# Two mixers of a three-layer network: pooled features made feature-major, moving sums by shifted additions in place of band matmuls

## The chip, the cores and the metric

One core of a Trainium2 chip runs the whole program. The time is device microseconds for one execution; lower is better. TensorE multiplies, VectorE, ScalarE and GpSimd (called POOL in the rows) do elementwise work, and SP issues most of the loads.

## The reference, cut to what matters

The network has two hybrid layers and a third of another kind, on 256 tokens and 1024 features, in float32. The change is in the first two layers' mixers, in the projection u and the pooling of it:

```python
h = rms_norm(x, mix_norm)
z = h @ w_in
u, q, k, v, gl = z[..., :512], z[..., 512:1024], ...
y_pool = multiscale_pool(u, pool_w, pool_scale)
y_attn = moba_attention(rope(rms_norm(q)), rope(rms_norm(k)), v)
merged = gates[0] * (y_pool @ w_branch_pool) + gates[1] * (y_attn @ w_branch_attn)

def multiscale_pool(u, w_grp, scale):      # u: 256 tokens, 4 groups of 128 features
    for g, w in enumerate((2, 4, 8, 16)):
        lo = max(t + 1 - w, 0)             # causal moving mean over w tokens
        mean = (csum[t + 1, g] - csum[lo, g]) / (t + 1 - lo)
    d = pooled - u
    y = einsum('bsgc,gcd->bsgd', d, w_grp) # a 128x128 product per group
    return y * scale
```

## The kernel before

Every weight matrix comes in tiles of 128 x 1024 (512 KB), in the order of `tile_plan`. Each tile is split into a high and a low part: ScalarE copies it to `whi` with rounding (L1362), VectorE subtracts that from the tile and writes `wlo` (L1971). A product is then three matmuls, high x high, high x low and low x high. Six split tiles exist at a time. ScalarE works at most five tiles ahead of TensorE and VectorE four (`ahead`; three or so in the gates), and a new tile may take a buffer when TensorE has finished the tile six before it.

There are two forms of product. `group` (by `group_part`, L760, L761, L765) makes the result token-major: 256 tokens are two halves `a`, each with a PSUM bank of 512 feature columns, and one weight tile serves two of the eight input blocks. `feat_block` (L723, L724, L730) makes it feature-major: the weight tile is the stationary side, the 256 tokens are the columns, and one tile gives 128 features over all eight input blocks. The wide form (L739, L746) is that of the gates.

A mixer of layer 0 or 1 (`mixer1`) runs the groups k, q, u, v (four tiles each) and then sixteen gate tiles, the two branch products and the output product. TensorE, ScalarE and VectorE each have their own program and go through the same tiles; in each of them `tick` counts beats, two to a tile, so that q holds beats 1 to 8, u 9 to 16, v 17 to 24 and the gates begin with 25. Small work is hung on the beats. In the kernel before:

- beats 10 and 12: TensorE transposes k (L1062), ScalarE evicts it (L1693). Beats 20 and 22: the same for q (L1691).
- beats 11 and 13: VectorE multiplies q by the cosine table (L2295), 15 and 16: it adds the sine part (L2324), which GpSimd has made in four products (L2661, L2662), after a few small operations for the norm (L2666 to L2674).
- beats 17, 19, 21, 23 (`pool_diff`): TensorE multiplies the token-major `us` with band matrices (`poolm`, 1536 columns of constants), which gives the mean minus u, feature-major (L1108, L1109), in float32. ScalarE evicts it to `dT` (L1699).
- beats 18, 20, 22, 24 (`pool_mix`): TensorE multiplies `dT` with the group's 128x128 matrix (L1118), ScalarE evicts the high part with the scale (L1705), VectorE the low part (L2328, semaphore `yplo`).
- beat 26: the first attention scores on TensorE (L998); they wait for all four `yplo`.

`pool_mix(g)` writes bank `side[2 + g % 2]`, so groups 2 and 3 wait until VectorE has evicted groups 0 and 1:

```python
if g >= 2:
    E.wait_ge("yplo", 4 * l + g - 1)
```

Each engine goes through its program in order; an instruction that waits holds all behind it on its engine. The order of a VectorE `tick` before the change is: q by cosine, q addition, `pool_mix`, attention.

Of the kernel before, what the change touches and what calls it, by code (L numbers as in the profile page):

```python
# [15 lines left out]
P = 128  # L16
S = 256
# [13 lines left out]
def constants():  # L31
    c = {}
    c["ident"] = np.eye(P, dtype=np.float32)
    t = np.arange(P)
    tri = np.where(t[None, :] > t[:, None], np.float32(NEG), np.float32(0)).astype(np.float32)
    c["cmask"] = np.concatenate([tri, np.zeros((P, P), np.float32), tri], 1)
    c["bigT"] = np.where(t[:, None] > t[None, :], np.float32(1e30), np.float32(0)).astype(np.float32)
    half = 32
    inv = (np.float32(1.0) / (np.float32(10000.0) ** (np.arange(half, dtype=np.float32) * np.float32(2.0 / 64)))).astype(np.float32)
    ang = (np.arange(S, dtype=np.float32)[:, None] * inv[None, :]).astype(np.float32)  # L40
    cos, sin = np.cos(ang).astype(np.float32), np.sin(ang).astype(np.float32)
    cs = np.concatenate([cos, cos], 1).reshape(2, P, 64)
# [3 lines left out]
    pm = []  # L46
    tt = np.arange(S)
    for w in (2, 4, 8, 16):
        lo = np.maximum(tt + 1 - w, 0)
        cnt = (tt + 1 - lo).astype(np.float32)  # L50
        s = np.arange(S)[:, None]
        m = np.where((s >= lo[None, :]) & (s <= tt[None, :]), np.float32(1) / cnt[None, :], np.float32(0))
        m = m - np.eye(S)
        pm += [m[0:P, :], m[P:S, P:S]]
# [100 lines left out]
def tile_plan():  # L155
# [100 lines left out]
class Counts:  # L256


    def __init__(self, plan):
# [31 lines left out]
        for st, tag in enumerate(STAGES):  # L291
            groups = [f"{tag}p"] if tag in FFNS else [tag + g for g in (("k", "q", "u", "v") if tag != "M" else ("k3", "nq", "v3", "mv", "mo"))]
# [25 lines left out]
    def banks(self):  # L318
# [37 lines left out]
        for st, tag in enumerate(STAGES):  # L356
# [20 lines left out]
            if tag != "M":  # L377
# [5 lines left out]
                for a in range(2):  # L383
                    claim((f"{tag}u", a), "u_ev", 2 * m + a + 1)
# [31 lines left out]
def build_program(nc, x_in, wstream, gains, const_in, par_in, out, cat, pat, plan, addends):  # L416
# [3 lines left out]
    with ExitStack() as ctx:  # L420
# [43 lines left out]
        kT1, v1, us = arena[:, 3328:4352], arena[:, 4352:5376], arena[:, 6400:7424]  # L464
        qT1 = arena[:, 2304:3328]
        dT, tab1, poolm, pw = arena[:, 7424:7680], arena[:, 7680:8192], arena[:, 8192:9728], arena[:, 9728:10240]
# [54 lines left out]
        PES = ["tile", "tok", "xt", "ft", "acc", "qkt_t", "pl_d", "pl_w", "score", "pT", "pv",  # L521
               "kT_t", "lg_row", "lg_col", "c_hT", "c_w2", "c_rep", "c_sc", "c_pT", "pv_c", "ml_s", "ml_h", "ml_t", "turn"]
        ACTS = ["w_hi", "sq", "xhi", "tok_a", "act", "hidhi", "pad", "qk_ev", "hst_sq", "kt_ev", "qt_ev", "u_ev", "v_ev", "dT", "yphi", "ex", "g_low",
                "pT_ev", "low", "yahi", "gate", "k3_ev", "kc2_ev", "kT_ev", "nq_ev", "v3_ev", "mqk_ev", "lg_ln", "lg_ex", "c_part", "c_hc",
                "c_kv", "c_exp", "c_pTe", "conv_t", "mv_ev", "ml_e", "ml_sq", "m_yhi", "mo_ev", "tokp", "tokv", "sil", "xf_hi"]
        DVES = ["sq_v", "xhi0", "w_lo", "x", "xn", "xlo", "tok_m", "mul", "hidlo", "cv", "mrg", "hst_rd", "rp_n", "rp_c", "rp_add", "yplo",
                "mx", "nrm", "g_sum", "yalo", "gfin", "sum", "lg_d", "lg_cp", "c_fold", "c_v", "c_s", "conv_q", "conv_k", "ml_k", "ml_p", "ml_d", "ml_n", "ml_g", "m_ylo", "gmo", "xf", "xf_lo", "comb", "tokm"]
        POOLS = ["mh", "rstd", "hb", "tab", "zero", "kst", "qst", "rp_s", "X", "warm", "cvp", "c_z", "ml_r", "padz", "rowz", "kz", "vz", "xz"]
# [71 lines left out]
        def sp_program(E):  # L600
# [88 lines left out]
        def pe_program(E):  # L689
# [393 lines left out]
            def mixer1(s, l):  # L1083
# [14 lines left out]
                def pool_diff(g):  # L1098
                    E.wait_ge("u_ev", 2 * l + 2)
                    E.wait_ge("ld_pw", 32 * l + 32)  # L1100
                    if g < 2:
                        E.wait_ge("kt_ev", 2 * l + g + 1)
                    else:
                        E.wait_ge("qt_ev", 2 * l + g - 1)
                        E.wait_ge("dT", 4 * l + g - 1)
                    b, pm = side[g % 2], poolm[:, g * 384:g * 384 + 384]
                    reach = P + 2 ** (g + 1)
# [4 lines left out]
                def pool_mix(g):  # L1112
                    E.wait_ge("dT", 4 * l + g + 1)
                    if g >= 2:
                        E.wait_ge("yplo", 4 * l + g - 1)
                    else:
                        E.wait_ge("x", 4 * (s - 1) + 3 + g)
                    e.matmul(side[2 + g % 2][:, 0:S], pw[:, g * P:g * P + P], dT, start=True, stop=True).then_inc(sem["pl_w"], 1)  # L1118

                def before(i):  # L1120
                    if i < 2:
                        E.wait_ge("dT", 4 * l + 3 + i)
                        E.wait_ge("kt_ev", 2 * l + 2)
                        E.wait_ge("qt_ev", 2 * l + 2)
                        E.wait_ge("yplo", 4 * l + 4)
                    else:
                        E.wait_ge("v_ev", 2 * l + 2)

                def tick():
# [6 lines left out]
                    if beat in (17, 19, 21, 23):  # L1136
                        pool_diff((beat - 17) // 2)
# [5 lines left out]
                for g in ("q", "u", "v"):  # L1143
                    group(f"{tag}{g}", 512, tick)
# [193 lines left out]
        def act_program(E):  # L1338
# [329 lines left out]
            def mixer1(s, l):  # L1668
# [26 lines left out]
                def pool_diff(g):  # L1695
                    E.wait_ge("pl_d", 4 * l + g + 1)
                    if g:
                        E.wait_ge("pl_w", 4 * l + g)
                    e.activation(dT, side[g % 2][:, 0:S], ACT.Copy).then_inc(sem["dT"], 1)  # L1699

# [6 lines left out]
                def tick():  # L1707
# [6 lines left out]
                    if beat in (17, 19, 21, 23):  # L1714
                        pool_diff((beat - 17) // 2)
# [7 lines left out]
                for g in ("q", "u", "v"):  # L1723
                    for k0, _ in a_group(512):
# [5 lines left out]
                    for a in range(2):  # L1730
# [4 lines left out]
                        if g == "u":  # L1735
                            e.activation(us[:, a * 512:a * 512 + 512], b[:, :], ACT.Copy).then_inc(sem["u_ev"], 1)
                        else:
                            e.activation(v1[:, a * 512:a * 512 + 512], b[:, :], ACT.Copy).then_inc(sem["v_ev"], 1)
# [223 lines left out]
        def dve_program(E):  # L1962
# [334 lines left out]
            def mixer1(s, l):  # L2297
# [27 lines left out]

                def pool_mix(g):
# [4 lines left out]
                def tick():  # L2331
# [18 lines left out]
                for g in ("q", "u", "v"):  # L2350
                    for k0, _ in a_group(512):
# [279 lines left out]
        def pool_program(E):  # L2631
# [67 lines left out]
            def prepare1(s, l):  # L2699
# [6 lines left out]
                e.tensor_scalar(hb16, PR(f"bg{l}"), 0.5, None, ALU.mult).then_inc(sem["hb"], 1)  # L2706
                rope_tables(tab1[:, 0:256], PR(f"kn{l}"), 1, 2 * l + 1)
# [149 lines left out]
def pack_weights(I, plan, addends, total):  # L2857
# [37 lines left out]
    for l in range(2):  # L2895
# [3 lines left out]
        for j, nm in enumerate("uqkv"):  # L2899
            group(f"L{l}{nm}", wi[:, j * 512:(j + 1) * 512])  # L2900
# [96 lines left out]
```

## Time and profile before

| what | value |
|---|---|
| median of 3 runs | 1406.26 us (1406.22 to 1406.81) |
| the profiled execution | 1406.52 us, span 1404.5 us |
| granted TensorE clock, mean | 1.000 |
| busy: TensorE matmul, VectorE, ScalarE, GpSimd | 1398.6, 1089.2, 862.0, 229.6 us |
| instructions | 20175 |

The span is the time from the first to the last instruction in the profile; the profiled execution took 2.0 us more than it. Matmuls overlap, so a matmul's own duration is longer than the step from its start to the next one's; steps are the measure of what it costs.

### The profile page before, as it was taken

To read this page: it belongs to the slowest core of one execution; us is meant where nothing else is said; L and a number is where in the kernel's file an instruction comes from. 1 tells how busy PE (TensorE), PEld (TensorE's weight loads), DVE (VectorE), ACT (ScalarE), POOL (GpSimd) and SP (SyncE) were. 2 spreads that over 40 slices of the span, in tenths; PEclk is the share of its full clock that TensorE was granted. 3 is DMA by queue.
4 is the path that set the end of the run, shared out by engine and by line. 5 is a ranking of instruction groups with operands and counts; after the bars stand their busy time and mean duration, and the time that the engine had idled before them with its cause. 6 is when DMAs were issued, how large, how long until landed. Compare 5 with 4: busy or idle time off the path is not lost.

```text
span 1404.5 us, 20175 instructions
## 1 busy us (share of the span) xinstructions
PE 1398.6 (100%) x7624; PEld 1195.2 (85%) x7624; DVE 1089.2 (78%) x1650; ACT 862.0 (61%) x1397; POOL 229.6 (16%) x307
## 2 busy tenths in 40 slices
PE   9999999999999999999999999999999999999999
PEld 7888888898888888888888888888888899888887
DVE  7878876776978878788775778788777878678776
ACT  6657656755657657675567646666567765455553
POOL 1112133000111001112050001114149200100000
PEclk9999999999999999999999999999999999999999
DMA  9999755464999859998564557999547336456551
GB/s 369 301 299 279 220 204 176 136 197 180 304 258 289 211 190 300 273 273 223 194 223 149 169 181 270 267 275 259 188 154 250 126 121 216 160 174 216 192 185 58
DMA packets 84200, 305.75 MB, mean 218 GB/s; under 512 B 9348, under 2 KB 9480, under 8 KB 84104
## 3 DMA queue, kind: packets, MB, share of 16 engines
q1 hardware_dynamic: 69992, 253.33, 50.8%
q0 software_dynamic: 13824, 50.34, 18.8%
q8 instruction: 61, 1.00, 0.3%
q10 hardware_dynamic: 288, 0.79, 0.2%
q14 instruction: 35, 0.29, 0.1%
HBM read 303.37 MB, written 1.05 MB: 217 GB/s over the span
## 4 chain that ended last, share of the span: by engine, by line
PE 98%; DVE 1%; DMA 0%; ACT 0%; issue 0%; POOL 0%; DVEq 0%; ACTq 0%; POOLq 0%
PE bank L739 18%; PE bank L746 9%; PE bank L693 9%; PE bank L694 9%; PE bank L695 9%; PE bank L899 5%; PE bank L898 5%; PE bank L902 5%; PE bank L760 4%; PE bank L765 4%; PE bank L761 4%; PE bank L723 3%; PE bank L730 3%; PE bank L724 3%; PE bank L713 1%; PE bank L998 1%
## 5 line engine op out<-in xcount | busy, mean ns | idle before, releaser
L1971 DVE TENSOR_TENSOR wlo<-raw,whi 128x1024 fp32r<-128x1024 f32 x409 | 492.2, 1231 | 12.3 <-ACT whi L1362 12.2
L1362 ACT ACTIVATE whi<-raw 128x1024 fp32r<-128x1024 f32 x409 | 417.5, 1048 | 19.0 <-PE bank L695 12.4
L739 PE MATMUL bank<-hx,whi 128*128 128x512 f32 x1088 | 268.6, 393 | 0.0
L739 PEld LDWEIGHTS bank<-hx,whi 128*128 128x128 f32 x1088 | 200.4, 188 | 41.3 <-issue 2.0
L693 PE MATMUL bank<-whi,hid 128*128 128x512 f32 x536 | 211.1, 394 | 0.0
L694 PE MATMUL bank<-wlo,hid 128*128 128x512 f32 x536 | 209.2, 390 | 0.0
L695 PE MATMUL bank<-whi,hid 128*128 128x512 f32 x536 | 208.8, 389 | 0.0
L746 PEld LDWEIGHTS bank<-hx,wlo 128*128 128x128 f32 x1088 | 142.9, 191 | 7.7
L746 PE MATMUL bank<-hx,wlo 128*128 128x256 f32 x1088 | 145.2, 282 | 0.0
L1971 DVE TENSOR_TENSOR wlo<-gates,whi 128x1024 fp32r<-128x1024 f32 x96 | 116.1, 1221 | 5.6 <-ACT whi L1362 5.1
L695 PEld LDWEIGHTS bank<-whi,hid 128*128 128x128 f32 x536 | 100.6, 188 | 21.4
L1362 ACT ACTIVATE whi<-gates 128x1024 fp32r<-128x1024 f32 x96 | 100.5, 1056 | 26.8 <-PE bank L695 13.8
L693 PEld LDWEIGHTS bank<-whi,hid 128*128 128x128 f32 x536 | 100.9, 188 | 18.9
L694 PEld LDWEIGHTS bank<-wlo,hid 128*128 128x128 f32 x536 | 100.9, 188 | 18.4
L1391 ACT ACTIVATE hid<-prod 128x256 fp32r<-128x256 f32 x78 | 32.6, 418 | 122.0 <-DVE prod L2280 58.6
L2683 POOL DMA_DIRECT2D gates<-w_dram x64 | 56.0, 874 | 288.0 <-DVE wlo L1971 287.6
L760 PE MATMUL bank<-whi,hx 128*128 128x512 f32 (+1 forms) x256 | 101.9, 399 | 0.9 <-DVE hx L1999 0.9
L761 PE MATMUL bank<-whi,hx 128*128 128x512 f32 (+1 forms) x256 | 98.1, 384 | 0.0
L765 PE MATMUL bank<-wlo,hx 128*128 128x512 f32 (+1 forms) x256 | 77.4, 385 | 0.0
L2638 POOL TENSOR_SCALAR small<-small 128x1 f32<-128x1 f32 x15 | 10.7, 716 | 403.5 <-ACT arena L1377 403.5
L898 PE MATMUL bank<-whi,yhi 128*128 128x512 f32 x192 | 75.2, 392 | 0.0
L899 PE MATMUL bank<-whi,ylo 128*128 128x512 f32 x192 | 74.9, 390 | 0.0
(298 smaller groups left out, 2375.0 us busy)
## 6 DMA issues: line engine op xcount, KB each, us to landing
raw<-w_dram SPq DMA_DIRECT2D x414, 512.0 KB, 4.5
gates<-w_dram POOLq DMA_DIRECT2D x64, 512.0 KB, 8.0
gates<-w_dram SPq DMA_DIRECT2D x32, 512.0 KB, 5.5
arena<-w_dram POOLq DMA_DIRECT2D x32, 512.0 KB, 9.0
arena<-w_dram SPq DMA_DIRECT2D x16, 512.0 KB, 5.1
gain<-g_dram SPq DMA_DIRECT2D x7, 512.0 KB, 3.3
arena<-c_dram SPq DMA_DIRECT2D x2, 768.0 KB, 6.2
out_dram<-x SPq DMA_DIRECT2D x4, 256.0 KB, 2.0
```

The costliest lines, as they stand in the source:

```text
L693: e.matmul(psum, shi, mhi, start=first, stop=False, skip_group_check=True)
L694: e.matmul(psum, shi, mlo, start=False, stop=False, skip_group_check=True)
L695: return e.matmul(psum, slo, mhi, start=False, stop=last, skip_group_check=True)
L739: e.matmul(b[:, :], hi_of(j)[:, k * P:k * P + P], hx[:, k * 2 * S:k * 2 * S + 2 * S], start=k == 0, stop=False, skip_group_check=True)
L746: ins = e.matmul(b[:, 0:S], lo_of(j)[:, k * P:k * P + P], hiT(k), start=False, stop=k == KD - 1, skip_group_check=True)
L760: e.matmul(b[:, 0:n], hiT(k, a * P, a * P + P), w, start=k == 0, stop=False, skip_group_check=True)
L761: e.matmul(b[:, 0:n], loT(k, a * P, a * P + P), w, start=False, stop=False, skip_group_check=True)
L765: ins = e.matmul(b[:, 0:n], hiT(k, a * P, a * P + P), w, start=False, stop=k == KD - 1, skip_group_check=True)
L898: e.matmul(b[:, :], sh(k), half(hi_of(j), k), start=k == 0 and n not in (2, 4), stop=False, skip_group_check=True)
L899: e.matmul(b[:, :], sl(k), half(hi_of(j), k), start=False, stop=False, skip_group_check=True)
L1362: e.activation(hi_of(t), raw_of(t), ACT.Copy).then_inc(sem["w_hi"], 1)
L1971: e.tensor_tensor(lo_of(t), raw_of(t), hi_of(t).bitcast(F32), ALU.subtract).then_inc(sem["w_lo"], 1)
```

## The change

The u projection becomes feature-major: four tiles of one group of 128 features each, by `feat_block`, evicted by ScalarE to `u4`, 16 columns of zeros ahead of the 256 tokens of each group. VectorE makes the moving sums from it by repeated doubling: a sum over 2 is u plus u shifted by 1, a sum over 4 that plus itself shifted by 2, and so on, so group g needs g + 1 additions. A small product mends the first w tokens, whose mean is over fewer, and a last operation takes sum / w minus u and writes it into `u4`, where TensorE's `pool_mix` reads it. The band matmuls, their evictions and their constants go. On VectorE the new `pool_diff(g)` is hung on beats 12, 14, 16 and 18, behind the q work of the beat and ahead of `pool_mix`. GpSimd sets the zeros in the stage before.

```diff
@@ constants
-    c["pool"] = np.concatenate(pm, 1).astype(np.float32)
+    tt = np.arange(16)
+    c["pool"] = np.broadcast_to(np.concatenate([np.float32(w) / np.minimum(tt + 1, w).astype(np.float32) for w in (2, 4, 8, 16)])[None, :], (P, 64)).astype(np.float32)
@@ tile_plan
+            if g == "u":
+                plan.extend((f"L{l}u{f}", TW, True) for f in range(4))
+                continue
@@ banks
-                for a in range(2):
-                    claim((f"{tag}u", a), "u_ev", 2 * m + a + 1)
+                for f in range(4):
+                    claim((f"{tag}u", f), "u_ev", 4 * m + f + 1)
@@ SP, load_pool_w
-                e.dma_start(poolm, const_in[:, cat["pool"][0]:cat["pool"][1]]).then_inc(sem["ld_pw"], 16)
+                e.dma_start(poolc, const_in[:, cat["pool"][0]:cat["pool"][1]]).then_inc(sem["ld_pw"], 16)
@@ TensorE, mixer1
-                def pool_diff(g):
-                    ...
-                    e.matmul(b[:, 0:reach], us[:, g * P:g * P + P], pm[:, 0:reach], start=True, stop=False, skip_group_check=True)
-                    e.matmul(b[:, P:S], us[:, 512 + g * P:512 + g * P + P], pm[:, S:S + P], start=False, stop=True,
-                             skip_group_check=True).then_inc(sem["pl_d"], 1)
                 def pool_mix(g):
-                    E.wait_ge("dT", 4 * l + g + 1)
+                    E.wait_ge("pl_d", PLD(l, g))
...
-                    e.matmul(side[2 + g % 2][:, 0:S], pw[:, g * P:g * P + P], dT, start=True, stop=True).then_inc(sem["pl_w"], 1)
+                    e.matmul(side[2 + g % 2][:, 0:S], pw[:, g * P:g * P + P], u4[:, g, 16:16 + S], start=True, stop=True).then_inc(sem["pl_w"], 1)
...
-                for g in ("q", "u", "v"):
-                    group(f"{tag}{g}", 512, tick)
+                group(f"{tag}q", 512, tick)
+                for f in range(4):
+                    feat_block(T[f"{tag}u{f}"], claim((f"{tag}u", f))[:, 0:S], tick=tick)
+                group(f"{tag}v", 512, tick)
@@ ScalarE, mixer1
+                        for f in range(4):
+                            ahead(T[f"{tag}u{f}"])
+                            tick()
+                            tick()
+                            E.wait_ge("tile", DONE[f"{tag}u{f}"])
+                            E.wait_ge("uz", l + 1)
+                            e.activation(u4[:, f, 16:16 + S], bank[K.BANK[f"{tag}u", f][0]][:, 0:S], ACT.Copy).then_inc(sem["u_ev"], 1)
@@ VectorE, mixer1
+                def pool_diff(g):
+                    n = PLD(l, g) - (g + 3)
+                    u, s_ = u4[:, g, :], u4[:, g, :]
+                    E.wait_ge("u_ev", 4 * l + g + 1)
...
+                    for i in range(g + 1):
+                        d, o = 2 ** i, part_sum[i % 2]
+                        if n:
+                            E.wait_ge("pl_d", n)
+                        e.tensor_tensor(o[:, 2 * d - 1:], s_[:, 2 * d - 1:], s_[:, d - 1:16 + S - d], ALU.add).then_inc(sem["pl_d"], 1)
+                        s_, n = o, n + 1
+                    w = 2 ** (g + 1)
+                    E.wait_ge("ld_pw", 32 * l + 32)
+                    E.wait_ge("pl_d", n)
+                    e.tensor_tensor(s_[:, 16:16 + w], s_[:, 16:16 + w], poolc[:, 16 * g:16 * g + w], ALU.mult).then_inc(sem["pl_d"], 1)
+                    E.wait_ge("pl_d", n + 1)
+                    e.scalar_tensor_tensor(u[:, 16:], s_[:, 16:], 1.0 / w, u[:, 16:], ALU.mult, ALU.subtract).then_inc(sem["pl_d"], 1)
...
+                    if beat in (12, 14, 16, 18):
+                        pool_diff((beat - 12) // 2)
                     if beat in (18, 20, 22, 24):
                         pool_mix((beat - 18) // 2)
@@ GpSimd, prepare1
+                if l:
+                    E.wait_ge("pl_w", 4 * l)
+                e.memset(u4[:, :, 0:16], 0.0).then_inc(sem["uz"], 1)
```

## Rows read from the trace of the kernel before

**Rows 1.** The page, busy time of each engine, and its chain that ended last by engine.

```profile
PE 1398.6 (100%) x7624; PEld 1195.2 (85%) x7624; DVE 1089.2 (78%) x1650; ACT 862.0 (61%) x1397; POOL 229.6 (16%) x307
...
PE 98%; DVE 1%; DMA 0%; ACT 0%; issue 0%; POOL 0%; DVEq 0%; ACTq 0%; POOLq 0%
```

**Rows 2.** Windows (u, v; v of layer 1): length, busy PE, PEld, DVE, ACT, POOL, clock, DMA.

```profile
210.69:222.52 11.83, 11.83 (x58) 9.72 (x56) 11.04 (x13) 7.00 (x10) 7.57 (x9) 1.00 0.59 180
222.52:237.81 15.29, 15.29 (x81) 12.97 (x80) 8.63 (x10) 8.33 (x14) 4.93 (x7) 1.00 0.57 198
...
728.13:743.43 15.30, 15.30 (x82) 12.97 (x80) 8.58 (x10) 8.33 (x14) 4.88 (x7) 1.00 0.56 193
```

**Rows 3.** TensorE in order of time, layer 0: start us, us.

```profile
221.16 0.39 PE L760 MATMUL bank<-whi,hx 128*128 128x512 f32 x1
...
222.52 0.39 PE L760 MATMUL bank<-whi,hx 128*128 128x512 f32 x1
...
225.70 0.59 PE L1118 MATMUL bank<-arena 128*128 128x256 f32 x2
...
233.90 0.60 PE L1118 MATMUL bank<-arena 128*128 128x256 f32 x2
...
237.81 2.19 PE L739 MATMUL bank<-hx,whi 128*128 128x512 f32 x8
...
240.88 1.58 PE L998 MATMUL bank<-arena 64*128 64x128 f32 x16
```

**Rows 4.** TensorE in order of time, branch products of layer 0.

```profile
292.19 0.28 PE L723 MATMUL bank<-yhi,whi 128*128 128x256 f32 x1
...
293.63 0.28 PE L723 MATMUL bank<-yhi,whi 128*128 128x256 f32 x1
```

**Rows 5.** ScalarE in order of time, layer 0.

```profile
217.69 0.58 ACT L1693 ACTIVATE arena<-bank 128x512 f32<-128x512 f32 x1
```

**Rows 6.** VectorE's groups by line and form: busy us, mean ns.

```profile
L2122 DVE TENSOR_TENSOR prod<-sil,prod 128x256 f32<-128x256 f32 x32 | 13.6, 425 | 4.2
...
L2276 DVE SCALAR_TENSOR_TENSOR sil<-gates,bank 128x256 f32<-128x256 f32 x24 | 10.0, 417 | 11.3 <-PE bank L730 11.0 <-issue 0.3
...
L2223 DVE TENSOR_TENSOR small<-small 128x2 f32<-128x2 f32 x32 | 5.7, 180 | 1.1
```

**Rows 7.** VectorE in order of time, layer 0: start us, us.

```profile
207.19 0.68 DVE L2307 TENSOR_TENSOR gates<-gates,small 128x512 f32<-128x512 f32 x1
207.90 0.69 DVE L2295 TENSOR_TENSOR gates<-gates,arena 128x512 f32<-128x512 f32 x1
208.51 1.77 DVE L1971 TENSOR_TENSOR wlo<-raw,whi 128x1024 fp32r<-128x1024 f32 x1
...
219.81 0.69 DVE L2295 TENSOR_TENSOR gates<-gates,arena 128x512 f32<-128x512 f32 x1
220.41 1.22 DVE L1971 TENSOR_TENSOR wlo<-raw,whi 128x1024 fp32r<-128x1024 f32 x1
...
225.82 1.20 DVE L2324 TENSOR_TENSOR gates<-gates 128x512 f32<-128x512 f32 x1 [2.45 <-POOL gates L2662]
...
228.26 1.22 DVE L1971 TENSOR_TENSOR wlo<-raw,whi 128x1024 fp32r<-128x1024 f32 x1
229.40 0.48 DVE L2328 SCALAR_TENSOR_TENSOR ylo<-bank,par,yhi 128x256 fp32r<-128x256 f32 x1
```

**Rows 8.** GpSimd in order of time, layer 0.

```profile
207.95 1.25 POOL L2661 TENSOR_TENSOR gates<-gates,arena 128x256 f32<-128x256 f32 x1 [0.30 <-DVE gates L2307]
...
220.67 1.06 POOL L2666 TENSOR_SCALAR small<-small 128x8 f32<-128x8 f32 x1
...
224.36 0.74 POOL L2661 TENSOR_TENSOR gates<-gates,arena 128x256 f32<-128x256 f32 x1
...
226.43 1.19 POOL L2662 TENSOR_TENSOR gates<-gates,arena 128x256 f32<-128x256 f32 x1
```

**Rows 9.** TensorE in order of time, the kernel's start.

```profile
9.74 0.50 PE L760 MATMUL bank<-whi,hx 128*128 128x512 f32 x1 [0.91 <-DVE hx L1999]
```

More of the change, by code:

```diff
@@ L45, in constants @@
     c["sin"] = sn.transpose(1, 0, 2).reshape(P, 128)
[L46 to L54, printed above, removed]
-    c["pool"] = np.concatenate(pm, 1).astype(np.float32)
+    tt = np.arange(16)
+    c["pool"] = np.broadcast_to(np.concatenate([np.float32(w) / np.minimum(tt + 1, w).astype(np.float32) for w in (2, 4, 8, 16)])[None, :], (P, 64)).astype(np.float32)
     n = np.arange(15)
@@ L291, in __init__ @@
         for st, tag in enumerate(STAGES):
-            groups = [f"{tag}p"] if tag in FFNS else [tag + g for g in (("k", "q", "u", "v") if tag != "M" else ("k3", "nq", "v3", "mv", "mo"))]
+            groups = [f"{tag}p"] if tag in FFNS else [tag + g for g in (("k", "q", "v") if tag != "M" else ("k3", "nq", "v3", "mv", "mo"))]
             for g in groups:
@@ L463, in build_program @@
                [[arena[:, 10240:10624], arena[:, 10624:11008]]] * 2 + [[arena[:, 4864:5248], arena[:, 5248:5632]]]]
-        kT1, v1, us = arena[:, 3328:4352], arena[:, 4352:5376], arena[:, 6400:7424]
+        kT1, v1 = arena[:, 3328:4352], arena[:, 4352:5376]
         qT1 = arena[:, 2304:3328]
-        dT, tab1, poolm, pw = arena[:, 7424:7680], arena[:, 7680:8192], arena[:, 8192:9728], arena[:, 9728:10240]
+        tab1, poolc, pw = arena[:, 7680:8192], arena[:, 9280:9344], arena[:, 9728:10240]
+        u4 = arena[:, 8192:9280].rearrange("p (g y) -> p g y", y=16 + S)
+        part_sum = [arena[:, 6400 + i * (16 + S):6400 + (i + 1) * (16 + S)] for i in range(2)]
+        PLD = lambda l, g: 18 * l + sum(i + 3 for i in range(g + 1))
         ks, qs, tmp, ro = (gates[:, i * 1024:i * 1024 + 1024] for i in range(4))
@@ L520, in build_program @@
                 + ["st", "ml_r4", "ml_m"])
-        PES = ["tile", "tok", "xt", "ft", "acc", "qkt_t", "pl_d", "pl_w", "score", "pT", "pv",
+        PES = ["tile", "tok", "xt", "ft", "acc", "qkt_t", "pl_w", "score", "pT", "pv",
                "kT_t", "lg_row", "lg_col", "c_hT", "c_w2", "c_rep", "c_sc", "c_pT", "pv_c", "ml_s", "ml_h", "ml_t", "turn"]
-        ACTS = ["w_hi", "sq", "xhi", "tok_a", "act", "hidhi", "pad", "qk_ev", "hst_sq", "kt_ev", "qt_ev", "u_ev", "v_ev", "dT", "yphi", "ex", "g_low",
+        ACTS = ["w_hi", "sq", "xhi", "tok_a", "act", "hidhi", "pad", "qk_ev", "hst_sq", "kt_ev", "qt_ev", "u_ev", "v_ev", "yphi", "ex", "g_low",
                 "pT_ev", "low", "yahi", "gate", "k3_ev", "kc2_ev", "kT_ev", "nq_ev", "v3_ev", "mqk_ev", "lg_ln", "lg_ex", "c_part", "c_hc",
                 "c_kv", "c_exp", "c_pTe", "conv_t", "mv_ev", "ml_e", "ml_sq", "m_yhi", "mo_ev", "tokp", "tokv", "sil", "xf_hi"]
-        DVES = ["sq_v", "xhi0", "w_lo", "x", "xn", "xlo", "tok_m", "mul", "hidlo", "cv", "mrg", "hst_rd", "rp_n", "rp_c", "rp_add", "yplo",
+        DVES = ["sq_v", "xhi0", "w_lo", "x", "xn", "xlo", "tok_m", "mul", "hidlo", "cv", "mrg", "hst_rd", "rp_n", "rp_c", "rp_add", "yplo", "pl_d",
                 "mx", "nrm", "g_sum", "yalo", "gfin", "sum", "lg_d", "lg_cp", "c_fold", "c_v", "c_s", "conv_q", "conv_k", "ml_k", "ml_p", "ml_d", "ml_n", "ml_g", "m_ylo", "gmo", "xf", "xf_lo", "comb", "tokm"]
-        POOLS = ["mh", "rstd", "hb", "tab", "zero", "kst", "qst", "rp_s", "X", "warm", "cvp", "c_z", "ml_r", "padz", "rowz", "kz", "vz", "xz"]
+        POOLS = ["mh", "rstd", "hb", "tab", "zero", "kst", "qst", "rp_s", "X", "warm", "cvp", "c_z", "ml_r", "padz", "uz", "rowz", "kz", "vz", "xz"]
         sem = {s: ctx.enter_context(nc.semaphore(f"s_{s}")) for s in DMAS + PES + ACTS + DVES + POOLS}
@@ L1096, in turn_qk, with pool_mix @@
                     turn4([ro[:, a * 512 + c * P:a * 512 + c * P + P] for c in range(4)], side[a]).then_inc(sem["qkt_t"], 1)
-                def pool_diff(g):
-                    E.wait_ge("u_ev", 2 * l + 2)
+                def pool_mix(g):
+                    E.wait_ge("pl_d", PLD(l, g))
                     E.wait_ge("ld_pw", 32 * l + 32)
[L1101 to L1107, printed above, removed]
-                    e.matmul(b[:, 0:reach], us[:, g * P:g * P + P], pm[:, 0:reach], start=True, stop=False, skip_group_check=True)
-                    e.matmul(b[:, P:S], us[:, 512 + g * P:512 + g * P + P], pm[:, S:S + P], start=False, stop=True,
-                             skip_group_check=True).then_inc(sem["pl_d"], 1)
-                def pool_mix(g):
-                    E.wait_ge("dT", 4 * l + g + 1)
                     if g >= 2:
@@ L1117, in pool_mix @@
                         E.wait_ge("x", 4 * (s - 1) + 3 + g)
-                    e.matmul(side[2 + g % 2][:, 0:S], pw[:, g * P:g * P + P], dT, start=True, stop=True).then_inc(sem["pl_w"], 1)
+                    e.matmul(side[2 + g % 2][:, 0:S], pw[:, g * P:g * P + P], u4[:, g, 16:16 + S], start=True, stop=True).then_inc(sem["pl_w"], 1)
                 def before(i):
                     if i < 2:
-                        E.wait_ge("dT", 4 * l + 3 + i)
                         E.wait_ge("kt_ev", 2 * l + 2)
@@ L1135, in tick @@
                         turn_qk((beat - 20) // 2, True)
-                    if beat in (17, 19, 21, 23):
-                        pool_diff((beat - 17) // 2)
                     if beat in (18, 20, 22, 24):
@@ L1693, in turned @@
                         e.activation(tok(kT1), by4(side[a][:, :]), ACT.Copy).then_inc(sem["kt_ev"], 1)
[L1695 to L1699, printed above, removed]
                 def pool_mix(g):
@@ L1713, in tick @@
                         turned((beat - 20) // 2, 1)
-                    if beat in (17, 19, 21, 23):
-                        pool_diff((beat - 17) // 2)
                     if beat in (18, 20, 22, 24):
@@ L1723, in mixer1 @@
                 for g in ("q", "u", "v"):
+                    if g == "u":
+                        for f in range(4):
[5 more added lines that the diff above has]
+                            e.activation(u4[:, f, 16:16 + S], bank[K.BANK[f"{tag}u", f][0]][:, 0:S], ACT.Copy).then_inc(sem["u_ev"], 1)
+                        continue
                     for k0, _ in a_group(512):
@@ L1734, in mixer1 @@
                         E.wait_ge("tok", K.TOK[f"{tag}{g}"]) if a == 0 else E.wait_ge("tile", K.TOKTILE[f"{tag}{g}"])
[L1735 to L1738, printed above, removed]
+                        e.activation(v1[:, a * 512:a * 512 + 512], b[:, :], ACT.Copy).then_inc(sem["v_ev"], 1)
                 for f in range(KD):
@@ L2324, in add @@
                     e.tensor_tensor(sl5(ro, a), sl5(ro, a), sl5(tmp, a), ALU.add).then_inc(sem["rp_add"], 1)
+                def pool_diff(g):
+                    n = PLD(l, g) - (g + 3)
+                    u, s_ = u4[:, g, :], u4[:, g, :]
+                    E.wait_ge("u_ev", 4 * l + g + 1)
+                    if l == g == 0:
+                        E.wait_ge("ld_c", 16)
+                    for i in range(g + 1):
[10 more added lines that the diff above has]
+                    e.scalar_tensor_tensor(u[:, 16:], s_[:, 16:], 1.0 / w, u[:, 16:], ALU.mult, ALU.subtract).then_inc(sem["pl_d"], 1)
                 def pool_mix(g):
@@ L2350, in mixer1 @@
                 for g in ("q", "u", "v"):
-                    for k0, _ in a_group(512):
+                    for k0 in range(4) if g == "u" else [k for k, _ in a_group(512)]:
                         ahead(T[f"{tag}{g}{k0}"])
@@ L2899, in pack_weights @@
         for j, nm in enumerate("uqkv"):
-            group(f"L{l}{nm}", wi[:, j * 512:(j + 1) * 512])
+            if j:
+                group(f"L{l}{nm}", wi[:, j * 512:(j + 1) * 512])
+        for f in range(4):
+            src[f"L{l}u{f}"] = lambda wi=wi, f=f: kmajor(wi[:, f * P:(f + 1) * P])
         for f in range(KD):
```

## The prediction

> **What bounds the kernel now.** I read the page first: TensorE is busy for the whole span and carries 98% of the chain that ended last, while VectorE is busy 78% [rows 1]. So a step of this change counts if it takes time out of TensorE's stream or makes TensorE wait; whatever else moves is free as long as TensorE doesn't notice.
>
> Then I read the stretch around the change, in windows and in order of time. In layer 0 the product u runs from 210.69 to 222.52 us and v from 222.52 to 237.81. In the u window VectorE is busy 11.04 of 11.83 us and GpSimd 7.57; in the v window VectorE is busy only 8.63 of 15.29 [rows 2]. Layer 1 is the same picture 505.6 us later (its v window starts at 728.13 and lasts 15.30 us [rows 2]), so one layer is worked out and doubled. The reader is to see that the room on VectorE lies behind u, while four of its new pieces of work are asked for in u or at the first beat of v.
>
> **TensorE's own terms.** Products. A u block of 6 matmuls of 512 columns takes 222.52 - 221.16 = 1.36 us [rows 3], so the eight blocks of u take 10.9. After the change u is four feature blocks of 24 matmuls of 256 columns. Twelve such matmuls of the same helper, L723 to L730, take 293.63 - 292.19 = 1.44 us [rows 4], so 96 take 11.52: **0.6 us more**, because 256 columns take 0.120 us and not half of 0.227.
> Band matmuls. From 222.52 to 225.70 lie two blocks (2.72) and the first pool_diff, which so costs 0.46 us [rows 3]. Four go: **1.84 us less**, three of them (1.38) ahead of pool_mix(2). pool_mix, the q and k transposes and the beats at which they stand are unchanged.
> If nothing waits, a layer is 1.84 - 0.6 = 1.24 us shorter.
>
> **Other engines.** ScalarE drops four evictions of dT and two of us and gains four of 256 columns; it sits in front of nothing new. The first of them stands behind its k eviction at 217.69 [rows 5], so it is done at about 218.6, before VectorE asks at 220.41; the others follow as TensorE finishes each block. With two more banks claimed, v now takes those of u0 and u1, which are evicted by 220.3, long before 223.1. The constants' transfer on SP's queue shrinks from 1536 columns to 64 per layer, in the place it had, and no transfer is on the chain [rows 1]. The memset of the margins is one more GpSimd instruction in the stage before, ahead of the rope tables, whose products come tens of microseconds later. TensorE waits for neither, so both are 0; uncovered, the memset would cost some tenths at the head of GpSimd's tables and the smaller transfer would gain nothing.
>
> **VectorE's new work, per layer.** Ten shifted additions of 257 to 271 columns. A tensor-tensor operation of 256 columns from SBUF takes 0.425 us [rows 6]; the step from 256 to 512 columns (0.685) is 0.26, so 271 columns take 0.44. Each waits for the one before. Such a waited step starts 0.03 us after the end of its producer (207.19 + 0.68 to 207.90), where steps without a wait start 0.08 before it [rows 7]. So the additions take 0.47 each at most, 4.67 together. The four small multiplications are 0.18 + 0.03 [rows 6], 0.84 together. The four closing subtractions take 0.42 with a constant as scalar [rows 6] (0.48 is the other end, that of L2328 at 229.40 with a scalar from SBUF [rows 7]), less the 0.08 overlap: 1.36. The sum is **6.87 us**: 1.02, 1.49, 1.95 and 2.41 for the four groups.
>
> **Where it lands.** TensorE's pool_mix(2) reuses the bank of pool_mix(0), and waits until VectorE has evicted that (yplo). VectorE's program has this eviction behind all four pool_diffs: at beat 18 pool_diff(3) stands first. Now it is done at 229.88 [rows 7] and pool_mix(2) runs at 233.90 [rows 3], 4 us of slack. After:
> TensorE would be there at 233.90 + 0.6 - 1.38 = 233.1.
> VectorE, from 220.41 (the end of the first q product by the cosine, unchanged): three splits of 1.14 (v2, v3, g00; 1.22 less the overlap) 3.42; q by cosine 0.60; two rope additions 1.20; the four groups 6.87; the eviction 0.48. That ends at 220.41 + 12.57 = 232.98, which is just in time.
> But GpSimd stands between. Its first rope product at 207.95 took 1.25 us, that at 224.36 with VectorE idle 0.74 [rows 8]; and VectorE's split at 208.51 took 1.77 and not 1.22, its addition at 225.82 1.20 and not 0.69 [rows 7]. The starts and ends fit one rule: instructions with two operands in SBUF take turns with GpSimd's, each for its whole length. GpSimd's four q products (224.36 to 227.62 [rows 8]) now meet an idle VectorE for most of their time. After the change VectorE has work all through, and must sit out four turns of 0.66 us (0.74 less the overlap of 0.08) and two short ones of 0.1: **2.8 us**. VectorE can't pass them, since its rope additions at beats 15 and 16 need their results and stand ahead of pool_diff(2) and (3).
> So pool_mix(0) is evicted at about 235.8. A TensorE that starts again after a wait shows 0.50 us for a matmul of 0.39 [rows 9]: +0.1, pool_mix(2) effectively at 235.95. From there to the gates it took 237.81 - 233.90 = 3.91 [rows 3], less one pool_diff: 3.45. The gates begin at 239.4 and not 237.81: **+1.6 us a layer**. The 0.6 us of the products does not enter, being inside the wait.
> With the turns the eviction is at 235.8; were the two engines only to share bandwidth, with no turns, it would be at 232.98 and the layer 1.24 us shorter. The Trainium skill (SBUF — State Buffer, "Who interferes with whom") names turns of just this kind, for a VectorE instruction with two SBUF inputs against a GpSimd one that reads SBUF; all eighteen new instructions have two. It is a page's rule against this change, and this trace agrees with it (1.77 against 1.22).
>
> **Behind it.** VectorE then does split, pool_mix(1), split, pool_mix(2), split: 1.14, 0.40, 1.14, 0.40, 1.14 after 235.7, to 239.9; pool_mix(3) on TensorE at 239.1 needs only pool_mix(1) of it (237.3). TensorE's first scores, 3.07 us into the gates, come at 242.5 and need the last eviction, at about 240.6. The late splits (g10 at 236.8) are ready before the gates use them, and the loads that wait for them are four tiles ahead. Nothing is queued on.
> The transposed q at beat 20 needs the first rope addition, now at about 229.1 and not 227.0, when TensorE arrives at 229.0: a wait of 0.1 to 0.2, which the later one swallows.
>
> **Sum.** Two layers, +3.2 us. The profiled execution took 1406.52 us (span 1404.5 and 2.0 around it), which gives 1409.7; it lies 0.26 above the median of the three runs, 1406.26, from which I state the forecast: **1409.5 us**. A change below 0.2% (2.8 us) can't be told from none here.
>
> **Rivals.**
> (a) No wait: VectorE is in time and TensorE keeps its 1.24 us a layer: 1403.8. For it: without the turns VectorE would be in time by 0.1 us. Against: of VectorE's stretch 2.7 us must go for that (235.8 to 233.1), and 1.5 before the change gains at all; it decides from an eviction before 234.3.
> (b) The waited steps cost nothing extra. For it: little; the row at 207.90 shows 0.71 from start to start where unwaited ones have 0.60 [rows 7]. Fourteen such steps at 0.11 are 1.5 us, the eviction is at 234.3 and a layer comes out even: 1406.5. The Trainium skill, VectorE: DVE Perf Modes, "The DRAIN you can't avoid", says that a semaphore between VectorE operations costs nothing; the row disagrees, and I go by the row.
> (c) A larger wait: subtractions at 0.48 and small products at 0.25 add 0.5, and a longer turn for each of GpSimd's short instructions (1.06 us is what the one at 220.67 took while a split ran [rows 8]) up to 1.0: eviction at 237.3, +3.1 a layer, 1412.5. A wait of 2.7 us on TensorE is also long beside the 5.9 us that it idles in the whole span [rows 1]; if the granted clock (1.00 in both windows, the 2.4 GHz level) fell to the 1.2 GHz level until the gates, 3.4 us would take 6.8.
> (d) The change does not do what it says: nothing speaks for this.
>
> **Chances.** Main case 0.72, with a range of its own from 1408.0 to 1411.5 (1.6 a layer give or take 0.7 to 1.0); of it 0.45 above 1409.07, the bound, and 0.27 within. (c) 0.12, slower. (b) 0.07, within. (a) 0.09, at -0.18%, so 0.06 within and 0.03 faster. Together faster 0.03, same 0.40, slower 0.57. The range leaves out (a) and the far end of (c): 1404.5 to 1412.5.
>
> **What the profile after would show.** u longer by 0.6 us; no idle in TensorE up to beat 22 of v beyond some tenths; then one wait of 2 to 3 us at pool_mix(2) in each layer, released by VectorE's L2328 (by its new number). VectorE busy almost without a gap from u's start to the end of v, its operations in groups of 0.44, and some of them at 1.0 to 1.2 us where GpSimd's rope products stand. If pool_mix(2) does not wait, the turns or the prices of the additions are wrong. If a wait stands elsewhere, at the transposed q or at the first scores, the order I followed is wrong.

## The result, and the profile after

| kernel | median us | lowest to highest | runs |
|---|---|---|---|
| before | 1406.49 | 1406.01 to 1406.89 | 16 |
| after | 1409.22 | 1406.87 to 1410.76 | 16 |

The ratio is 1.0016, with a 95% interval of 1.0010 to 1.0023: slower by 2.7 us, which the interval tells from no change, though the value lies inside the bound of 0.2%. The forecast was 1409.5. The runs of the changed kernel spread over 3.9 us where those of before spread over 0.9, and that spread has a cause of its own, which the trace shows below.

First the page of the changed kernel: span and TensorE's share, and the chain by engine, which answers to [rows 1]. VectorE's part of the chain has gone from 1% to 4%.

```profile
span 1407.5 us, 20355 instructions
...
PE 1396.7 (99%) x7688; PEld 1197.1 (85%) x7688; DVE 1102.5 (78%) x1686; ACT 859.2 (61%) x1393; POOL 229.7 (16%) x309
...
PE 94%; DVE 4%; issue 1%; ACT 1%; DMA 1%; SPq 0%; DVEq 0%; ACTq 0%
```

Who TensorE waited for, in all; the longest alone is shown (pool_mix(2); two waits, one in each layer):

```profile
PE bank L1103 <- DVE ylo L2329: 3.9, 2, 2.0
```

TensorE in order of time, layer 0, from the transposed q at beat 22 (this profile runs 0.2 us later than that of before from the start of the kernel on). These lines answer to [rows 3]:

```profile
232.83 0.60 PE L1060 MATMUL bank<-cst,gates 128*128 128x128 f32 x4
235.38 0.67 PE L1103 MATMUL bank<-arena 128*128 128x256 f32 x2 [1.96 <-DVE ylo L2329]
235.70 0.69 PE L758 MATMUL bank<-whi,hx 128*128 128x512 f32 x1
236.19 0.63 PE L759 MATMUL bank<-whi,hx 128*128 128x512 f32 x1
236.62 0.63 PE L758 MATMUL bank<-whi,hx 128*128 128x512 f32 x1
...
239.54 0.40 PE L759 MATMUL bank<-whi,hx 128*128 128x512 f32 x1
239.78 0.63 PE L763 MATMUL bank<-wlo,hx 128*128 128x512 f32 x2
240.24 0.59 PE L1103 MATMUL bank<-arena 128*128 128x256 f32 x2
240.49 2.21 PE L737 MATMUL bank<-hx,whi 128*128 128x512 f32 x8
```

The wait stands where it was forecast, at pool_mix(2), released by the eviction of pool_mix(0). Behind it the matmuls of 512 columns go in steps of 0.43 us (236.19 to 236.62) and not 0.227, until 239.5. In layer 1 the same wait, as long, is followed by full speed:

```profile
742.99 0.67 PE L1103 MATMUL bank<-arena 128*128 128x256 f32 x2 [1.94 <-DVE ylo L2329]
743.31 0.58 PE L758 MATMUL bank<-whi,hx 128*128 128x512 f32 x1
743.73 0.40 PE L759 MATMUL bank<-whi,hx 128*128 128x512 f32 x1
743.96 0.39 PE L758 MATMUL bank<-whi,hx 128*128 128x512 f32 x1
```

The windows show it as granted clock (the columns are length, busy time of PE, PEld, DVE, ACT and POOL, then clock, DMA share, GB/s). The first is u, the next two run from pool_mix(2) to the gates in layers 0 and 1, the same work:

```profile
210.89:223.27 12.38, 12.38 (x106) 12.37 (x104) 11.45 (x15) 7.33 (x12) 8.03 (x10) 1.00 0.54 183
...
235.38:240.49 5.11, 5.11 (x17) 4.11 (x17) 4.05 (x5) 1.42 (x2) 0.00 (x0) 0.67 0.45 152
742.99:746.49 3.50, 3.50 (x17) 2.93 (x17) 3.50 (x5) 1.42 (x2) 0.00 (x0) 1.00 0.40 136
```

The window of layer 0 has a mean clock of 0.67: most of it at the 1.2 GHz level. The drop costs 5.11 - 3.50 = **1.6 us**. Cut finer, the clock was still 1.00 in the last 1.08 us of the wait, and fell when TensorE had begun again:

```profile
234.30:235.38 1.08, 0.00 (x0) 0.03 (x1) 1.05 (x4) 0.00 (x0) 0.00 (x0) 1.00 0.73 296
235.38:237.00 1.62, 1.61 (x5) 1.33 (x6) 1.62 (x3) 0.91 (x2) 0.00 (x0) 0.70 0.00 0
```

Each timed run comes with its mean clock over the span. Of the 16, six have 1.000 (1406.87 to 1408.45, median 1407.45), seven 0.999 (median 1409.49) and three 0.998 (median 1409.76, highest 1410.76). The profiled drop lost 0.33 x 5.11 = 1.7 us of clock, 0.0012 of 1407. So six runs had no drop and seven had one. The three at 0.998 lost twice as much, in two drops or in one twice as long; their times, only 0.3 us above the seven in the median, do not tell which. That makes 10 to 13 drops in 32 waits.

The starts of TensorE's same instructions in the two traces lie 0.2 us apart ahead of layer 0's mixer, 2.67 at its gates (1.6 of it the clock), 2.35 ahead of layer 1's mixer and 3.06 at its gates, which is the whole difference of the spans, 3.0. The wait alone so costs 0.9 us in layer 0 and 0.7 in layer 1.

VectorE in order of time, which answers to [rows 7]: from the first group of sums to the eviction that TensorE waits for.

```profile
220.59 0.43 DVE L2318 TENSOR_TENSOR arena<-arena 128x271 f32<-128x271 f32 x1
...
223.41 0.91 DVE L2318 TENSOR_TENSOR arena<-arena 128x271 f32<-128x271 f32 x2
224.35 0.59 DVE L2323 TENSOR_TENSOR arena<-arena 128x4 f32<-128x4 f32 x1
224.97 0.92 DVE L2325 SCALAR_TENSOR_TENSOR arena<-arena 128x256 f32<-128x256 f32 x1
225.82 1.75 DVE L1953 TENSOR_TENSOR wlo<-raw,whi 128x1024 fp32r<-128x1024 f32 x1
227.49 1.83 DVE L2306 TENSOR_TENSOR gates<-gates 128x512 f32<-128x512 f32 x2
229.25 1.37 DVE L2318 TENSOR_TENSOR arena<-arena 128x271 f32<-128x271 f32 x3
...
231.20 1.22 DVE L1953 TENSOR_TENSOR wlo<-raw,whi 128x1024 fp32r<-128x1024 f32 x1
232.33 1.84 DVE L2318 TENSOR_TENSOR arena<-arena 128x271 f32<-128x271 f32 x4
...
234.76 0.48 DVE L2329 SCALAR_TENSOR_TENSOR ylo<-bank,par,yhi 128x256 fp32r<-128x256 f32 x1
```

The third group takes 231.20 - 229.25 = 1.95 us and the fourth 234.76 - 232.33 = 2.43 with GpSimd idle, within 0.02 us of what was priced (1.95 and 2.41). The second takes 2.41 and not 1.49: its small product shows 0.59 us for what alone takes 0.17 to 0.2, its closing subtraction 0.92 for 0.42. GpSimd's four products of q with the sine table, which answer to [rows 8], stand beside just these (its starts and ends are rough):

```profile
223.91 1.02 POOL L2664 TENSOR_TENSOR gates<-gates,arena 128x256 f32<-128x256 f32 x1
224.88 0.74 POOL L2665 TENSOR_TENSOR gates<-gates,arena 128x256 f32<-128x256 f32 x1
225.58 0.91 POOL L2664 TENSOR_TENSOR gates<-gates,arena 128x256 f32<-128x256 f32 x1
226.45 1.72 POOL L2665 TENSOR_TENSOR gates<-gates,arena 128x256 f32<-128x256 f32 x1
```

The last of them took 1.72 us, most of it beside a split that ended at 225.82 + 1.75 = 227.57, and the two rope additions behind that split (227.49) then took 1.83 where 1.28 is their own (GpSimd's turns taken away, below). No instruction of VectorE is longer than alone where GpSimd's short ones stand. Whether these are turns is tested below.

### The profile page after: what moved, and what is told of

Same layout as the page of the kernel before. It is cut to its first block, busy times and chain, and to the rows that moved or that the text cites. A ratio compares the mean times of both kernels' runs of the same rounds, so it can differ in the third digit from the quotient of the medians.

```text
span 1407.5 us, 20355 instructions
## 1 busy us (share of the span) xinstructions
PE 1396.7 (99%) x7688; PEld 1197.1 (85%) x7688; DVE 1102.5 (78%) x1686; ACT 859.2 (61%) x1393; POOL 229.7 (16%) x309
## 4 chain that ended last, share of the span: by engine, by line
PE 94%; DVE 4%; issue 1%; ACT 1%; DMA 1%; SPq 0%; DVEq 0%; ACTq 0%
PE bank L737 18%; PE bank L744 9%; PE bank L691 9%; PE bank L692 9%; PE bank L693 9%; PE bank L896 5%; PE bank L897 5%; PE bank L900 5%; PE bank L721 3%; PE bank L728 3%; PE bank L722 3%; PE bank L758 3%; PE bank L759 3%; PE bank L763 3%; DVE wlo L1953 2%
## 5 line engine op out<-in xcount | busy, mean ns | idle before, releaser
L758 PE MATMUL bank<-whi,hx 128*128 128x512 f32 (+1 forms) x224 | 89.1, 399 | 1.1 <-DVE hx L1981 0.9
L759 PE MATMUL bank<-whi,hx 128*128 128x512 f32 (+1 forms) x224 | 86.3, 387 | 0.0
L763 PE MATMUL bank<-wlo,hx 128*128 128x512 f32 (+1 forms) x224 | 68.0, 386 | 0.0
```

The source lines that it names most:

```text
L758: e.matmul(b[:, 0:n], hiT(k, a * P, a * P + P), w, start=k == 0, stop=False, skip_group_check=True)
L759: e.matmul(b[:, 0:n], loT(k, a * P, a * P + P), w, start=False, stop=False, skip_group_check=True)
L763: ins = e.matmul(b[:, 0:n], hiT(k, a * P, a * P + P), w, start=False, stop=k == KD - 1, skip_group_check=True)
```

## The experiments

Theory A: the wait at pool_mix(2) for VectorE's eviction costs a layer 0.8 us (the mean of the two), net of what the matmuls save, and the clock drops are a consequence of that idle time. Its rivals: the loss lies in the 256-column products or in VectorE's load as such (B), and the drops come by chance (C). All medians below stand against 1406.39 (first four) or 1406.35 us (the other three) of the kernel before on the same chip; the changed kernel was not run again beside them, and its 1409.22 stands against 1406.49.

**VectorE evicts first at beat 18.**

```diff
 VectorE, tick
-                    if beat in (12, 14, 16, 18):
-                        pool_diff((beat - 12) // 2)
                     if beat in (18, 20, 22, 24):
                         pool_mix((beat - 18) // 2)
+                    if beat in (12, 14, 16, 18):
+                        pool_diff((beat - 12) // 2)
```

> At beat 18 VectorE evicts pool_mix(0) ahead of pool_diff(3) instead of behind it; nothing else is changed. Theory A (TensorE's wait at pool_mix(2) for that eviction is the whole loss, and the drop of the granted clock in layer 0 follows from the wait): the eviction ends at 232.8, TensorE arrives at 233.2, no wait there and about 0.4 us at pool_mix(3); each layer 0.9 to 1.0 us shorter than in the kernel before, no clock drop in any run, 1404.4 us. Theory B (the loss lies in the 256-column products or in VectorE's load as such, the order does not matter): 1408 to 1409 us. Theory C (the clock drops come by chance): runs still spread over 3 us.

Measured: 1404.60 us (1403.92 to 1405.17), ratio 0.9987 (0.9978 to 0.9996), clock 1.000 in all 11 runs. TensorE in order of time, layer 0: no wait at pool_mix(2), 0.30 at pool_mix(3) for the eviction of pool_mix(1).

```profile
232.94 0.60 PE L1103 MATMUL bank<-arena 128*128 128x256 f32 x2
...
236.58 0.67 PE L1103 MATMUL bank<-arena 128*128 128x256 f32 x2 [0.30 <-DVE ylo L2329]
```

Swapping two steps of VectorE's order, with the same work on every engine, turns a loss of 2.7 us into a gain of 1.8. So B falls.

**Own banks for pool_mix(2) and (3).**

```diff
 TensorE, ScalarE and VectorE, wherever pool_mix(g) writes or is evicted
-side[2 + g % 2][:, 0:S]
+side[(2, 3, 0, 1)[g]][:, 0:S]
 TensorE, pool_mix
                     if g >= 2:
-                        E.wait_ge("yplo", 4 * l + g - 1)
+                        E.wait_ge("qt_ev", 2 * l + g - 1)
```

> pool_mix(2) and (3) write the banks of the transposed q (evicted by then by ScalarE) instead of those of pool_mix(0) and (1), so TensorE no longer waits for VectorE's evictions; VectorE's order stays. Theory A: no wait at pool_mix(2) or (3), the layer 1.1 to 1.2 us shorter than before the change, at most 0.2 us of wait at the first scores: 1403.9 to 1404.2 us, without spread. Theory B: 1408 to 1409 us.

Measured: 1403.35 us (1402.94 to 1404.57), ratio 0.9979 (0.9970 to 0.9988), clock 1.000 in all 11. It is 0.55 us below the range expected. VectorE is as late as in the changed kernel (the eviction of pool_mix(0) starts at 234.60 here, there at 234.76), and it costs nothing:

```profile
233.12 0.60 PE L1103 MATMUL bank<-arena 128*128 128x256 f32 x2
...
236.30 0.59 PE L1103 MATMUL bank<-arena 128*128 128x256 f32 x2
236.54 2.21 PE L737 MATMUL bank<-hx,whi 128*128 128x512 f32 x8
```

The gates begin at 236.54 where they began at 237.81 [rows 3].

**The wait filled with idle matmuls.** The added products go into a free bank and are not used.

```diff
 TensorE, pool_mix
+                    if g == 2:
+                        E.wait_ge("qt_ev", 2 * l + 1)
+                        for _ in range(8):
+                            e.matmul(side[0][:, :], hiT(0, 0, P), hx[:, 0:2 * S], start=True, stop=True)
                     if g >= 2:
                         E.wait_ge("yplo", 4 * l + g - 1)
```

> TensorE runs eight matmuls of 512 columns (1.8 us) whose result nobody reads, into a free bank, ahead of its wait at pool_mix(2). Theory A with the clock drop as a consequence of the idle 2 us: the eviction still sets the end of v, so the wait costs the same 0.8 us a layer, but the granted clock stays 1.000 in every run: 1407.6 to 1407.9 us, spread under 1 us. Theory C (drops by chance): median near 1409 with the spread of 3 to 4 us. If the filler were on the path: 1410 or more.

Measured: 1407.48 us (1406.93 to 1408.82), ratio 1.0007 (0.9999 to 1.0016), clock 1.000 in all 11 runs. The median is 0.1 us below the range expected and the spread is 1.9 us, where under 1 was expected: the clock was not its only cause. In layer 0 pool_mix(2) still starts only when the eviction is done; the matmuls behind it go at full speed.

```profile
232.55 2.10 PE L1102 MATMUL bank<-hx 128*128 128x512 f32 x8
234.64 0.70 PE L1107 MATMUL bank<-arena 128*128 128x256 f32 x2
234.99 0.58 PE L758 MATMUL bank<-whi,hx 128*128 128x512 f32 x1
235.41 0.40 PE L759 MATMUL bank<-whi,hx 128*128 128x512 f32 x1
235.64 0.40 PE L758 MATMUL bank<-whi,hx 128*128 128x512 f32 x1
```

Sixteen useless matmuls make the changed kernel 1.7 us faster, and put it at the median of those of its runs that had no drop (1407.45). C falls: with the wait filled, 22 waits passed without a drop, where the changed kernel had 10 to 13 in its 32. Which of the waits are followed by a drop stays open.

**The sums left out.** Here VectorE only does the closing operation, on u itself; the moving mean is left out.

```diff
 VectorE, pool_diff
-                    for i in range(g + 1):
-                        ...
-                        e.tensor_tensor(o[:, 2 * d - 1:], s_[:, 2 * d - 1:], s_[:, d - 1:16 + S - d], ALU.add).then_inc(sem["pl_d"], 1)
-                        ...
-                    e.tensor_tensor(s_[:, 16:16 + w], s_[:, 16:16 + w], poolc[:, 16 * g:16 * g + w], ALU.mult).then_inc(sem["pl_d"], 1)
```

> VectorE leaves out the ten shifted additions and the four small products of each layer; only the closing operation is left, on u itself (the moving mean is left out). Theory A: VectorE is in time, TensorE keeps its own terms, 0.6 us more in u and 1.84 less in v: 1404.0 us (1403.7 to 1404.3). Theory B (the products cost more than the matmuls saved): 1406.5 or more.

Measured: 1403.19 us (1402.75 to 1404.19), ratio 0.9976 (0.9967 to 0.9986). TensorE's own terms, with VectorE costing nothing, were to give 1403.9 us (1406.39 less 2 x 1.24); the median is 0.7 below that and 0.5 below the range expected, and 0.3 to 0.5 of it lies outside the mixers (see "The products" below). Own banks come within 0.2 us of it with all the sums in place.

**GpSimd's turns taken away.** The four sine products of q work on 8 columns (`n` is 1 for q, one column of each of eight heads), so most of q's sine part is left out.

```diff
 GpSimd, rope_sin for q
-                    e.tensor_tensor(tv[:, k, :, 0:32], sv[:, k, :, 32:64], s1, ALU.mult)
-                    e.tensor_tensor(tv[:, k, :, 32:64], sv[:, k, :, 0:32], s2, ALU.mult)
+                    e.tensor_tensor(tv[:, k, :, 0:n], sv[:, k, :, 32:32 + n], s1[:, :, 0:n], ALU.mult)
+                    e.tensor_tensor(tv[:, k, :, 32:32 + n], sv[:, k, :, 0:n], s2[:, :, 0:n], ALU.mult)
```

> GpSimd's four products of q with the sine table per layer work on 8 columns instead of 256 (most of q's sine part is left out); VectorE's order and work are those of the changed kernel. Theory A1 (VectorE was late by the turns it took with GpSimd, 2.1 us by the trace): the eviction of pool_mix(0) ends near 233.2 as TensorE arrives, no wait over 0.3 us, no clock drop, 1403.5 to 1404.3 us. Theory A2 (VectorE is late by its own 6.9 us, the turns matter little): still a wait of 1.5 to 2 us, 1407 to 1409 us.

Measured: 1404.07 us (1403.33 to 1404.76), ratio 0.9983 (0.9974 to 0.9991). TensorE waits nowhere in the two mixers; pool_mix(2) starts at 232.97, 0.1 us behind the end of the eviction. VectorE in order of time, layer 0: the second group and the rope additions are back at their own prices.

```profile
220.16 0.43 DVE L2318 TENSOR_TENSOR arena<-arena 128x271 f32<-128x271 f32 x1
...
223.91 0.21 DVE L2323 TENSOR_TENSOR arena<-arena 128x4 f32<-128x4 f32 x1
224.15 0.42 DVE L2325 SCALAR_TENSOR_TENSOR arena<-arena 128x256 f32<-128x256 f32 x1
224.49 1.22 DVE L1953 TENSOR_TENSOR wlo<-raw,whi 128x1024 fp32r<-128x1024 f32 x1
225.64 1.28 DVE L2306 TENSOR_TENSOR gates<-gates 128x512 f32<-128x512 f32 x2
...
232.35 0.48 DVE L2329 SCALAR_TENSOR_TENSOR ylo<-bank,par,yhi 128x256 fp32r<-128x256 f32 x1
```

From the first addition to the eviction it is 232.35 - 220.16 = 12.19 us, in the changed kernel 234.76 - 220.59 = 14.17. The turns cost 2.0 us, and with all of VectorE's new work in place but without them the change is a gain. So both are needed for the loss: the 6.9 us alone just fitted.

**A longer wait.** Four more additions of 256 columns per layer, ahead of the eviction, results unused.

```diff
 VectorE, tick
                         pool_diff((beat - 12) // 2)
+                    if beat == 18:
+                        for i in range(4):
+                            E.wait_ge("pl_d", 22 * l + 18 + i)
+                            e.tensor_tensor(part_sum[0][:, 16:], part_sum[1][:, 16:], part_sum[1][:, 16:], ALU.add).then_inc(sem["pl_d"], 1)
```

> Four more additions of 256 columns on VectorE behind pool_diff(3) and ahead of the eviction of pool_mix(0), 1.8 us per layer, results unused. Theory A with the drop as a consequence of the idle time: the wait at pool_mix(2) grows from 1.95 to 3.8 us, +3.6 us in all, and the clock now drops in both layers in every run: 1406.4 + 1.2 + 3.6 + 3.5 = 1414.7 us with little spread. If the drops come by chance and not from the wait: +3.6 on 1409.2, 1412.8, with the same spread of 3 to 4 us. If VectorE's load there does not matter: 1409.

Measured: 1415.21 us (1414.42 to 1415.71, 5 runs), ratio 1.0061 (1.0048 to 1.0075); the mean clock is 0.996 in four runs and 0.997 in one. TensorE's pool_mix(2) in layer 0, and the granted clock of the 5 us behind it:

```profile
236.99 1.19 PE L1103 MATMUL bank<-arena 128*128 128x256 f32 x2 [3.77 <-DVE ylo L2329]
```

```profile
237.20:242.20 5.00, 5.00 (x12) 3.89 (x13) 3.83 (x5) 1.42 (x2) 0.00 (x0) 0.50 0.56 145
```

The matmul behind the wait takes 1.19 us where it took 0.67: here the clock is down before TensorE begins again. In layer 1 it fell only about when TensorE began again. The windows are one of layer 0's wait and two around the matmul of layer 1:

```profile
747.24 1.04 PE L1103 MATMUL bank<-arena 128*128 128x256 f32 x2 [3.76 <-DVE ylo L2329]
```

```profile
235.00:236.00 1.00, 0.00 (x0) 0.00 (x0) 0.92 (x3) 0.00 (x0) 0.00 (x0) 0.70 0.00 0
...
746.00:747.00 1.00, 0.00 (x0) 0.00 (x0) 0.97 (x3) 0.00 (x0) 0.00 (x0) 1.00 0.00 0
747.00:748.00 1.00, 0.76 (x3) 0.69 (x3) 1.00 (x2) 0.00 (x0) 0.00 (x0) 0.70 0.00 0
```

In this profile the clock was low about twice as long in layer 0 (until 242.2) as in layer 1 (until 750.8). With waits of 3.8 us it dropped in every run, and in the profiled one behind both; behind those of 1.95 us in 10 to 13 of 32 cases; behind those of 0.3 us (VectorE evicts first) in none of 22.

**Own banks and eviction first.** Both repairs together.

> Both repairs: pool_mix(2) and (3) in their own banks and VectorE's eviction ahead of pool_diff at beat 18. Theory A: nothing waits in either already with the banks alone, so the order adds nothing: 1403.2 to 1403.6 us, the same as with the banks alone. If VectorE's lateness at the first scores still cost something: 0.3 us less.

Measured: 1403.35 us (1403.09 to 1404.53), ratio 0.9981 (0.9972 to 0.9990), the same as with own banks alone. There was nothing left to wait for. The runs of this kernel lie in two groups, six from 1403.09 to 1403.35 and five from 1404.06 to 1404.53, all at clock 1.000; those of own banks do too (nine and two). The profile here is of a run at 1404.53 and has a wait of 0.43 us for ScalarE in the third layer (at 1077 us) that the profile of own banks, at 1403.45, does not have. Its cause was not looked for, and differences of some tenths between the repaired kernels are not read.

## Why the prediction was right, point by point

The place, the sign and the mechanism of the wait were right. That the size is right to 0.3 us (1409.5 and 1409.22; as a difference +3.2 and +2.7) is luck: two errors in it cancel, a wait priced at twice its cost and a drop of the clock left out.

- **The products.** u was to be 0.6 us longer; the windows show 12.38 against 11.83 [rows 2], 0.55. **The band matmuls and all of TensorE's own terms** were to give 1.24 us a layer. The kernel without sums is 3.2 us faster than before and its profile reaches the first gates 1.3 us earlier (236.68, on a profile that starts 0.2 later, against 237.81 [rows 3]). A further 0.3 to 0.5 us appears outside the mixers, in the second layer's first feed-forward stage, in every one of these kernels; a wait of 0.2 us for VectorE that the profile of before has there is gone. What removed it was not tried.
- **VectorE's prices** were right to a few hundredths, the 0.03 us behind each waited step included. Rival (b), by which waited steps are free, is wrong: the four additions of the fourth group go in 1.84 us, 0.46 each, where unwaited ones of 0.43 would take 0.35 each. The Trainium skill (VectorE: DVE Perf Modes, "The DRAIN you can't avoid") says, from a chain of eight copies, that a semaphore behind each costs nothing extra. These additions disagree, by 0.11 us each.
- **The turns** were the mis-sized term of the sum. I took 2.8 us, four whole products of GpSimd at 0.66 and two short ones. They measured 2.0. VectorE sat out about 0.5 us of each product: 0.42 (0.59 less 0.17), 0.50 (0.92 less 0.42), 0.53 (1.75 less 1.22) and 0.55 (the rope additions, 1.83 less 1.28), and nothing for the short ones. Why 0.5 and not the whole 0.66 no run here shows; in the records each delayed instruction has its own length left 0.13 to 0.16 us before the product beside it ends. The eviction ended at 235.04 on the clock of before and not 235.8, and the wait cost 0.9 us in layer 0 and 0.7 in layer 1 and not 1.6. The rule of the Trainium skill that I weighed (SBUF — State Buffer, "Who interferes with whom") is borne out in its main point: with GpSimd's products cut to 8 columns, VectorE's instructions take their own time again and TensorE does not wait.
- **The clock** I had only in rival (c), behind a wait of 2.7 us where 1.96 came, until the gates and at a cost of 3.4 us, and gave that rival 0.12 in all. By the mean clocks it happened in 10 to 13 of the 32 waits; the one that was profiled cost 1.6 us. Without it the forecast would have been too high by 2 us: the runs with no drop have a median of 1407.45, 1.0 us above before, which is 0.9 + 0.7 less the 0.3 outside the mixers, within 0.4 us. With it the median is 1409.22. Rival (c) was thus partly true and the main case partly false; the chances I gave them did not allow for both at once.
- **Behind it:** no further wait, as forecast. The 0.1 to 0.2 us at the transposed q did not come either: the rope addition was in time. The loads and the late splits did not show.
- **The range** of 1404.5 to 1412.5 holds all 16 runs.

## What to carry to other kernels

When work moves to an engine that was idle in the mean, look for what already stands behind it in that engine's own order. Here an eviction of 0.48 us had 4 us of slack, and its wait was for a bank; two free banks were worth 5.9 us between the medians, more than the matmuls that the change took away (1.84 us a layer). Price a second engine's turns together with the new work: without GpSimd's products the new work fitted, and without the sums GpSimd's products cost nothing that TensorE noticed. And a wait of TensorE is not priced by its length alone; those of 1.95 us also brought the clock down in 10 to 13 of 32 cases, those of 0.3 us in none of 22. The sign was a spread of runs, with a mean clock just below 1.000, that the kernel before did not have.

## What the runs showed of the hardware

The granted clock does not react to a wait of 1.95 us in one fixed way: in one profiled execution it fell behind the first such wait (mean 0.67 over 5.11 us) and not behind the second, equally long (1.00). Eight unused matmuls in the gap kept it up in all 11 runs (1407.48 us, against 1407.45 of the runs of the changed kernel without a drop). In the profile with waits of 3.8 us it had fallen before TensorE began again in layer 0 (0.70 in 235.00 to 236.00), and in layer 1 only about when TensorE began (1.00 in 746.00 to 747.00, 0.70 in the next).

Beside GpSimd's 128x256 products the narrow product of VectorE (0.59 us where 0.17 to 0.21 is its own) and its closing subtraction, a scalar_tensor_tensor with both inputs in SBUF (0.92 where 0.42), were held up by 0.42 to 0.50 us, about as much as the wide tensor-tensor operations (0.53 and 0.55). None of the shifted additions stood beside such a product in these traces.
